# Linear attention on one Trainium2 core: projection chunks regrouped between the decay levels, and the first level's products on one engine

## The reference, cut to what matters

```
S_t = diag(exp(g_t)) S_{t-1} + k_t^T v_t,  o_t = q_t S_t
att[t, s] = sum_d q[t, d] k[s, d] exp(cum[t, d] - cum[s, d])   for s <= t
```

## Time and profile before

| what | value |
|---|---|
| median of 3 runs | 1131.92 us (1127.45 to 1132.4) |
| the profiled execution | 1131.86 us |
| its span, first to last instruction | 1130.1 us |
| mean granted TensorE clock | 0.994 |
| PE busy | 1103.1 us (98%) |
| DVE, ACT, POOL busy | 730.2, 574.7, 451.6 us |

### The profile page before, as it was taken

The page is one execution under the profiler, slowest core; times in us unless marked ns, Lnnn a source line. Parts: engine busy times, 40 slices in busy tenths (PEclk is TensorE's granted clock), DMA queues, the critical chain, the costliest instruction groups (busy, mean ns, idle before and its releaser), DMA issues.

```text
span 1130.1 us, 23463 instructions
## 1 busy us (share of the span) xinstructions
PE 1103.1 (98%) x9169; PEld 1057.7 (94%) x9169; DVE 730.2 (65%) x1028; ACT 574.7 (51%) x824; POOL 451.6 (40%) x431
## 2 busy tenths in 40 slices
PE   7999999999999989999999999999999999999998
PEld 7896699999999769999999999998998989999997
DVE  6786658777555856777746665457747668777543
ACT  5547745555444664555534447644446445544433
POOL 4465614666302751666622112213433014666400
PEclk9999999999999999999999999998999999999999
DMA  9740147766555325666655554243334445766552
GB/s 289 239 150 2 64 123 215 191 185 187 173 187 168 113 76 149 186 186 186 186 169 172 173 177 132 80 148 100 125 112 139 160 112 149 188 185 184 187 181 80
DMA packets 226408, 175.40 MB, mean 155 GB/s; under 512 B 8720, under 2 KB 207632, under 8 KB 226208
## 3 DMA queue, kind: packets, MB, share of 16 engines
q1 hardware_dynamic: 225056, 173.00, 50.7%
q10 hardware_dynamic: 1248, 1.35, 0.4%
q0 software_dynamic: 32, 0.03, 0.0%
HBM read 173.32 MB, written 1.05 MB: 154 GB/s over the span
## 4 chain that ended last, share of the span: by engine, by line
PE 80%; DVE 6%; ACT 5%; issue 4%; POOL 3%; DMA 0%; DVEq 0%; SPq 0%; POOLq 0%; ACTq 0%
PE psum L624 24%; PE psum L630 24%; PE psum L625 23%; ACT work L1469 2%; PE psum L658 1%; ACT w_h L1330 1%; POOL work L2664 1%; PE psum L1176 1%; DVE w_l L1784 1%; DVE work L1981 1%; PE psum L1026 1%; POOL work L2668 1%; PE psum L652 1%; PE psum L748 1%; PE psum L775 0%
## 5 line engine op out<-in xcount | busy, mean ns | idle before, releaser
L624 PE MATMUL psum<-xh,w_h 128*128 128x256 f32 (+3 forms) x1760 | 439.4, 287 | 8.7 <-ACT w_h L1390 7.3
L625 PE MATMUL psum<-xl,w_h 128*128 128x256 f32 (+3 forms) x1760 | 433.2, 283 | 0.0
L624 PEld LDWEIGHTS psum<-xh,w_h 128*128 128x128 f32 (+1 forms) x1760 | 331.9, 189 | 12.7 <-ACT w_h L1390 7.3
L625 PEld LDWEIGHTS psum<-xl,w_h 128*128 128x128 f32 (+1 forms) x1760 | 332.8, 189 | 0.6
L1784 DVE TENSOR_TENSOR w_l<-raw,w_h 128x2048 fp32r<-128x2048 f32 (+2 forms) x91 | 202.6, 2226 | 141.6 <-ACT w_h L1330 141.6
L1330 ACT ACTIVATE w_h<-raw 128x2048 fp32r<-128x2048 f32 x92 | 167.8, 1824 | 202.9 <-PE psum L630 192.2
L630 PE MATMUL psum<-xh,w_l 128*128 128x256 f32 (+3 forms) x1760 | 246.0, 282 | 0.6 <-DVE w_l L1784 0.6
L630 PEld LDWEIGHTS psum<-xh,w_l 128*128 128x128 f32 (+1 forms) x1760 | 225.6, 189 | 1.0 <-DVE w_l L1784 0.8
L2560 POOL TENSOR_TENSOR work<-work 128x256 f32<-128x256 f32 x66 | 161.5, 2448 | 137.1 <-ACT work L1523 137.1
L2103 DVE TENSOR_TENSOR w_l<-raw,w_h 128x2048 fp32r<-128x2048 f32 x66 | 151.4, 2294 | 15.2 <-ACT w_h L1510 14.8
L624 PE MATMUL psum<-hid_h,w_h 128*128 128x256 f32 (+1 forms) x592 | 148.7, 282 | 1.0 <-DVE work L2428 0.7
(11 more groups left out here) (323 smaller groups left out, 1434.0 us busy)
## 6 DMA issues: line engine op xcount, KB each, us to landing
raw<-in_ffn_w_gu SPq DMA_DIRECT2D x88, 512.0 KB, 4.9
raw<-in_w_in SPq DMA_DIRECT2D x26, 1024.0 KB, 5.0
raw<-in_ffn_w_down SPq DMA_DIRECT2D x40, 512.0 KB, 4.5
raw<-in_w_ffn_up SPq DMA_DIRECT2D x22, 512.0 KB, 3.9
raw<-in_w_ffn_gate SPq DMA_DIRECT2D x22, 512.0 KB, 5.1
raw<-in_w_ffn_down SPq DMA_DIRECT2D x20, 512.0 KB, 4.3
raw<-in_nsa_w_in SPq DMA_DIRECT2D x9, 1024.0 KB, 5.2
raw<-in_swa_w_qkv SPq DMA_DIRECT2D x5, 1024.0 KB, 5.6
```

Of the source, the lines that this page charges most:

```text
L624: mm(dst, parts[0][:, k, cols], high, start=first, stop=False)
L625: mm(dst, parts[0][:, k, cols], low, start=False, stop=False)
```

## The change

- PE: one chunk (35) is put between level 0 and level 1, and the later groups are shifted by one: chunks 36 and 37 before level 2, 38 and 39 before level 3, up to 50 and 51 before level 9. No chunk stands after level 9. The number of chunks is the same.
- DVE: chunks 33 and 34 are taken between `distance(1)` and the first `low`, and no longer after `select(0)`. After `select(lv)` DVE takes, for lv >= 1, the chunks that stand before level lv on PE: 35 at lv = 1, 36 and 37 at lv = 2, up to 50 and 51 at lv = 9. `first_keys` and the semaphore `g_k_first` are gone.
- POOL: it multiplies queries and keys at level 1, as at the other levels.

```diff
--- before.py
+++ after.py
@@ -323,7 +323,7 @@
         z_scores, z_abs, z_relu, z_ln, z_soft, z_tri, z_weights, z_pv, z_out = map(sem, (
             "z_scores", "z_abs", "z_relu", "z_ln", "z_soft", "z_tri", "z_weights", "z_pv", "z_out"))
         g_log, g_x, g_abs, g_ln, g_cum = map(sem, ("g_log", "g_x", "g_abs", "g_ln", "g_cum"))
-        g_dist, g_decay, g_qk, g_k_first, g_att, g_sel = map(sem, ("g_dist", "g_decay", "g_qk", "g_k_first", "g_att", "g_sel"))
+        g_dist, g_decay, g_qk, g_att, g_sel = map(sem, ("g_dist", "g_decay", "g_qk", "g_att", "g_sel"))
         go_done, go_taken, go_sq, go_ss, go_root, go_inverse, go_spread, go_ready = map(sem, (
             "go_done", "go_taken", "go_sq", "go_ss", "go_root", "go_inverse", "go_spread", "go_ready"))
         gate_ready, mix_full, mix_high, mix_ready, z_high, go_full, go_high = map(sem, (
@@ -1235,8 +1235,6 @@
                     q, k = big2[:, 12:16, :], big2[:, 16:20, :]
                 else:
                     pe.wait_ge(g_qk, lv)
-                    if lv == 1:
-                        pe.wait_ge(g_k_first, 1)
                     q = g_q[:, lv % 2, :].rearrange("p (n t) -> p n t", n=GN)
                     k = g_k[:, lv % 2, :].rearrange("p (n t) -> p n t", n=GN)
                 if lv >= 2:
@@ -1270,10 +1268,8 @@
 
             level(0)
             for lv in range(1, TOP + 1):
-                if lv > 1:
-                    project2(31 + 2 * lv, 33 + 2 * lv)
+                project2(32 + 2 * lv if lv > 1 else 35, 34 + 2 * lv)
                 level(lv)
-            project2(51, 52)
             pe.wait_ge(g_sel, TOP + 1)
             for o in range(8):
                 n, dv = o // 2, o % 2
@@ -2356,25 +2352,17 @@
                     else:
                         line.put(V.copy_predicated(dst, each(mask.bitcast(U16), GN), src), sig)
 
-            def first_keys():
-
-                dve.wait_ge(g_decay, 1)
-                dst, k, d = (v.rearrange("p (q h) -> p q h", h=2)[:, :, 0]
-                             for v in (g_k[:, 1, :], big2[:, 16:20, :].rearrange("p n t -> p (n t)"), g_d[:, 1, :]))
-                line.put(V.tensor_tensor(dst, k, d, ALU.mult), g_k_first)
-
             line.settle()
             dve.wait_ge(late_loaded, 16)
             for lv in range(TOP + 1):
                 if lv < TOP:
                     distance(lv + 1)
+                    if lv == 0:
+                        take2(33, 35, split=False)
                     low(M_IN2 + 18 + lv)
-                if lv == 0:
-                    first_keys()
                 select(lv)
-                if lv < TOP:
-                    take2(33 + 2 * lv, 35 + 2 * lv, split=False)
-            take2(51, 52, split=False)
+                if lv:
+                    take2(32 + 2 * lv if lv > 1 else 35, 34 + 2 * lv, split=False)
 
             dve.wait_ge(gate_ready, 1)
             for o in range(8):
@@ -2662,9 +2650,7 @@
                 q, k = big2[:, 12:16, :].rearrange("p n t -> p (n t)"), big2[:, 16:20, :].rearrange("p n t -> p (n t)")
                 for n in ([None] if b <= 8 else range(GN)):
                     line.put(G.tensor_tensor(split(g_q[:, lv % 2, :], n)[:, :, 1, :], split(q, n)[:, :, 1, :],
-                                             split(d, n)[:, :, 1, :], ALU.mult), g_qk if lv == 1 else None)
-                    if lv == 1:
-                        continue
+                                             split(d, n)[:, :, 1, :], ALU.mult))
                     line.put(G.tensor_tensor(split(g_k[:, lv % 2, :], n)[:, :, 0, :], split(k, n)[:, :, 0, :],
                                              split(d, n)[:, :, 0, :], ALU.mult), g_qk if n in (None, GN - 1) else None)
```

## The result

The kernel after takes 1144.78 us (median of 4 runs, 1143.82 to 1147.19), the kernel before, on the same chip and with one run more, 1131.82. The ratio is 1.0128, 95% interval 1.0103 to 1.0154: slower, as forecast, inside the range of 1134 to 1149 and 2.7 us above the forecast. (Ratios and intervals in this text are those on record, estimated from all runs of both kernels; the quotient of the two medians is here 1.0115.) The profiled execution took 1143.83 us over a span of 1142.0.

The account below looks back on a forecast made before the run. TensorE (PE), busy 98% of the span, was taken as the bound, so only its idle or low-clock time counted: 1131.86 - 4.78 + 0.9 + 10.3 + 0.4 = 1138.7, plus 3.4 for clock falls, 1142.1 us; range 1134.0 to 1149.0.

Parts of the forecast that it names:

- The stop at level 1: PE's idle time between levels 0 and 1 (1.75 us) and the low clock behind it (3.03) vanish: 4.78 us gained.
- Level 1 waits for GpSimd: At level 1 PE waits for POOL's keys instead: 0.9 us, likely 0.6 to 1.3, outer bounds none and 4.1.
- the second of the two that the prediction named: One half of `distance(2)` goes ahead of POOL's level 1 keys, which are then ready at 774.5, not 773.8.
- The outer bound, 4.1: Longest wait at level 1, if POOL lets both distance halves and the next `low` pass: 4.1 us.
- The seven waits: Behind levels 2 to 8 PE waits for takes queued behind `select(lv)`: 1.9 + 6 x 1.4 = 10.3 us, bounds 3.8 and 13.3.
- let copy and `low` fit: Copy (1.9 us) and `low` (2.29) fit into the 2.93 + 2.12 us of chunk and level, so cost nothing.
- The stop ahead of the outputs: Behind level 9 no chunk hides `select(9)`, so PE starts the outputs 0.4 us late.
- The falls: Drops of PE's clock to 1.2 GHz behind the new stops: two at 1.7 us, 3.4 in all, bounds none and seven.
- The six short stops: PE's idle times of about 1.3 us behind levels 3 to 8, somewhat below the three stops seen in the trace.
- the one on the other side: Rival: PE's bank waits are met before levels 2 to 8 end; 1128.4 us, or 1127.1; chance 0.13.
- The case without falls: Rival: the six short stops leave PE's clock alone, so 1138.7 us; chance 0.2.
- The lower end of the range: 1134.0 us, given as the seven waits at about 0.7 us each and no fall of the clock.

Follow-up runs that it names:

- the two kernels with the takes early and GpSimd's keys: Kernel after with DVE's takes ahead of `select(lv)`: both of each pair, 1129.5 us (0.9993), or only the first, 1128.91 us (0.9989).
- the filled kernel: Kernel after plus seven extra bf16 matmuls of 384 columns, result unused, on PE behind each of levels 2 to 8: 1141.36 us, ratio 1.0092.
- the one with early takes: Kernel after with DVE's first take of each pair ahead of `low`, the second ahead of `select(lv)`; PE's order untouched: 1129.5 us, ratio 0.9993.
- the one with DVE's keys: Kernel after with both takes early, and DVE again multiplying level 1's keys, behind the first `low`: 1127.59 us, ratio 0.9969.

## Why the prediction was right

**The stop at level 1 goes, and its fall of the clock.** The prediction took 4.78 us for both and 0.9 of new wait. From level 0 to level 2 the kernel before takes 783.21 - 768.27 = 14.94 us; after, with a chunk more, 782.10 - 767.99 = 14.11. With 2.93 us for the chunk, 3.76 us were gained, against 3.88 forecast. The step held for this execution. As a gain over many it was too large: the two kernels with the takes early and GpSimd's keys have a stage 3.7 us shorter than the profiled execution of before, and yet ratios of 0.9993 and 0.9989, a gain of about 1 us. Of the difference 0.8 us is given back at the end of the span (below). No run shows what the rest is. A likely part: the 29 runs of before beside the second of them lie between 1128.37 us (mean clock 0.998) and 1134.36 (0.993), so the clock does not fall equally often in every execution, and the profiled one, with 0.994, is in the third with the lower clocks. Filling the stop in the kernel before gained no more than about 1 us either.

**Level 1 waits for GpSimd.** Forecast 0.9 (0.6 to 1.3), measured 0.71. The order was the second of the two that the prediction named, for which it had 1.3; the keys were ready at 773.96 in place of 774.5, and that the value in the middle came near is luck in part. (The outer bound, 4.1, leaves out the 0.15 us of release; with it the sum is 4.3.) POOL and DVE in the kernel after:

```profile
768.75 3.15 POOL L2652 TENSOR_TENSOR work<-big,work 128x544 f32<-128x544 f32 x1 [15.24 <-ACT work L1716]
771.87 2.09 POOL L2654 TENSOR_TENSOR work<-big,work 128x544 f32<-128x544 f32 x1
```

```profile
768.12 2.28 DVE L1780 TENSOR_TENSOR w_l<-raw,w_h 128x2048 fp32r<-128x2048 f32 x1
770.32 1.40 DVE L2351 TENSOR_TENSOR work<-psum,late_b 128x512 f32<-128x512 f32 x3
771.64 0.85 DVE L2320 TENSOR_TENSOR work<-work 128x544 f32<-128x544 f32 x1
772.41 2.13 DVE L2321 TENSOR_TENSOR work<-work 128x544 f32<-128x544 f32 x1
```

The queries end 1.5 us after `low`; one half of the distance goes first (0.85 us), then the keys, which end at 773.96, and only 0.6 us later the second half, which alone takes 0.7 and here 2.13. So in these rows the two engines take turns, one instruction each, and the one that waits is served next. "GPSIMD Engine Reference" of the Trainium skill, section "Specifications", has the contention between GpSimd and DVE instructions with two SBUF inputs, and the trace agrees; `select(0)` with one input from PSUM kept its 1.40 us beside POOL. The other rule that was weighed, elementwise work about twice as slow on GpSimd ("Performance versus the Vector engine", in the same page of the Trainium skill), agrees with the trace where no two-input work of DVE holds POOL up: its keys of levels 2 and 3 take 1.6 and 1.3 us against DVE's 0.7 for a distance of that size. It is not what decides here: at level 1 what counts is when each engine gets its turn. With the takes early, DVE's keys are 0.6 us better in the stage (68.63 to 68.04).

**The seven waits.** Forecast 10.3 us; the filled kernel against the one with early takes gives 10.6. The first wait is 1.70 us of idle time (forecast from 785.40 to 787.23, 1.83), those behind levels 3 and 4 1.30, behind 5 to 7 1.18. The last, 1.60, was costlier than its neighbours. The prediction let copy and `low` fit into a chunk and a level of 2.12 us; level 8 lasts 1.1 us and ended at 843.03, and `low` only at 843.52 (PE, then DVE):

```profile
841.89 1.14 PE L1249 MATMUL psum<-work 128*128 128x144 f32 x8
841.23 2.29 DVE L1780 TENSOR_TENSOR w_l<-raw,w_h 128x2048 fp32r<-128x2048 f32 x1 [3.45 <-ACT w_h L1326]
```

The stop ahead of the outputs was forecast at 0.4; it is 0.32 us long, and hiding it again saved 0.38 of the stage (68.04 to 67.66).

**The falls.** Forecast two at 1.7 us, 3.4; measured three at 1.5, 4.5, in this execution. This is the term that was mis-sized, in the number of falls. The six short stops had been set low because they are shorter than the 1.46 us of the earlier trace rows that left the clock alone; that does not hold: two of the three falls lie behind stops of 1.30 and 1.18 us, while equal stops behind levels 3, 6 and 7, and the longer one of 1.60 behind level 8, left the clock alone. The length of a stop does not tell whether a fall follows; what does stays open. By their times and clocks the two slower of the four runs probably had more than three; no profile shows them.

**What the prediction did not have.** Another 0.8 us lies behind the stage: 290.22 us from the first output matmul to the end of the span, against 289.46. It is no matmul's: from the last matmul's start to the end it is 5.8 us in the kernel before and 6.6 after, and the four stores of the output land later (median us from issue to landing, the last few us of the kernel before and of the kernel after):

```profile
out<-big SPq DMA_DIRECT2D x4, 256.0 KB, 2.3
```

```profile
out<-big SPq DMA_DIRECT2D x4, 256.0 KB, 2.7
```

It goes with the keys. In the profiles of all five kernels in which DVE multiplies them this last piece is 5.7 to 5.8 us, in all six with GpSimd's keys 6.6. The DMA views show something else that divides the kernels in the same way: one packet of the queue that the page calls `instruction`, by its name a piece of the program being loaded. In the five it comes from 5.2 to 4.2 us before the end of the span, as the first store starts; in the six from 3.2 to 2.4 us before it, in the middle of the last stores. Kernel before (1124.9 to 1125.9 us), kernel after (1138.8 to 1139.6):

```profile
q14 instruction: 1, 0.01, 2.6%
```

```profile
q14 instruction: 1, 0.01, 2.4%
```

And from 2.0 to 1.0 us before the end the stores still run at full rate in the five, while in the six they are nearly over but for a thin tail (200 to 206 packets against 73 to 80). Kernel before (1128.1 to 1129.1), kernel after (1140 to 1141):

```profile
DMA packets 200, 0.38 MB, mean 377 GB/s; under 512 B 16, under 2 KB 16, under 8 KB 200
```

```profile
DMA packets 78, 0.13 MB, mean 127 GB/s; under 512 B 16, under 2 KB 16, under 8 KB 78
```

So a likely cause is that an instruction more or less on an engine shifts the moment at which program is loaded, and that the load holds up a part of the last stores. That was not tried: it is argued from what goes together in eleven profiles. If it is so, the 0.8 us is an accident of the program's layout and not a price of GpSimd's products. Either way it comes with GpSimd's keys here, beside the 0.6 us of stage, and together they make 1.4 of the 1.9 us between the medians of the kernel with early takes (1129.5) and the one with DVE's keys (1127.59), which are of two sessions.

Of the rivals, the one on the other side (the takes are in time) is refuted by the seven rows of PE, and made true by the kernels that move the takes. The case without falls is what the filled kernel shows: its stage, 79.25 us, is 6.9 above the kernel before, as 1138.7 forecast. The rest of its profiled 1142.72 us lies outside the stage, part of it in a fall at 71 us that the profile of the kernel before does not have (granted clock 0.66 from 70.5 to 75.5 us, against 1.00). The lower end of the range was mis-added by a little: seven waits at 0.7 us each and no fall make 1133.3, not 1134.0, which changes nothing here.

## What to carry to other kernels

When the order of a producer is shifted against the consumer that frees its buffer, look at what stands ahead of the freeing instruction in the consumer's in-order queue: a take of 0.4 us behind the wrong `select` cost about 1.5 us seven times, and moving just that one instruction gave it all back. A wait that opens right behind a phase of small matmuls can cost again as lower clock, here 1.5 us a fall, behind three of seven. And a gain that one profiled execution shows as a fall of the clock should be counted at the rate at which it happens over many runs.

## What the runs showed of the hardware, beyond what was expected

- Stops of 1.18 and 1.30 us, behind a level of small matmuls, were followed by 3.4 us at 1.2 GHz in one place and by none in another of the same kernel; with seven bf16 matmuls of 384 columns in each of the seven stops the profile has no fall in the stage, and the four runs have mean clocks of 0.995 to 0.996 in place of 0.989 to 0.992.
- Slower matmuls can hide a wait: with the clock kept up in the kernel before, 0.41 us of waiting for POOL appeared at level 2.
- The same late takes cost 15 us in one grouping of the chunks and 41 us in the other, through the release of a weight slab two engines away.
- The last stores of the output ended 0.8 us later in every profile in which GpSimd multiplied level 1's keys, and in these alone one instruction load lies among the last stores; that the load is the cause is not shown.
